# Narrow bias tiles stored from buffers of their own, and seven-plus-one squares in the norms of a two-block transformer kernel

## The reference

```
cond = silu(c); mod = cond @ ada_w + ada_b            # shift, scale, gate
h = rms_norm(x, g) * (1 + scale) + shift              # before every mixer and every MLP
x = x + gate * mixer(h)                               # MLA, dilated, HGRN2 + RWKV7, Fourier + conv
x = x + gate * mlp(h)
rms_norm(x) = x / sqrt(mean(x*x) + eps) * g
```

## Time and profile before

| | us |
|---|---|
| median of 3 runs | 3524.82 (3521.92 to 3530.64) |
| profiled execution | 3524.06 |
| its span in the trace | 3522.1 |
| PE busy | 3307.0 (94%) |
| DVE busy | 1956.5 (56%) |
| POOL busy | 1273.3 (36%) |
| ACT busy | 1256.2 (36%) |

### The profile page before, as it was taken

One profiled execution on the slowest core, in us unless ns is written; L12 is line 12 of the kernel. 1 busy time (PEld: TensorE's weight loads), 2 busy tenths in 40 slices (PEclk: granted clock), 3 DMA queues, 4 the chain that ended last, 5 costly groups with the idle time before them and its releaser, 6 DMA issues.

```text
span 3522.1 us, 62638 instructions
## 1 busy us (share of the span) xinstructions
PE 3307.0 (94%) x25340; PEld 2564.3 (73%) x25340; DVE 1956.5 (56%) x2460; ACT 1256.2 (36%) x2175; POOL 1273.3 (36%) x729
## 2 busy tenths in 40 slices
PE   6799999999989999999999998888999999999998
PEld 4455678887766767778887887666678787578876
DVE  8457566554463555565565665454366465853344
ACT  3345432224554555522224433332322224242222
POOL 0044334445655544334443321000335443034442
PEclk9899999999999999999999998887999999999999
DMA  6433135443434333245442220000255343023322
GB/s 237 116 90 115 59 128 193 157 167 111 130 102 117 111 94 96 69 151 170 168 167 81 58 69 16 4 4 10 66 175 191 119 167 109 16 80 96 95 90 84
DMA packets 278074, 376.46 MB, mean 107 GB/s; under 512 B 59830, under 2 KB 204890, under 8 KB 266586
## 3 DMA queue, kind: packets, MB, share of 16 engines
q1 hardware_dynamic: 273496, 359.31, 32.2%
q10 hardware_dynamic: 4354, 13.98, 1.0%
HBM read 357.49 MB, written 15.73 MB: 106 GB/s over the span
## 4 chain that ended last, share of the span: by engine, by line
PE 77%; DVE 8%; issue 6%; DVEq 2%; ACT 2%; POOL 1%; DMA 1%; SPq 0%; ACTq 0%; POOLq 0%
PE ps L522 14%; PE ps L523 13%; PE ps L526 13%; PE ps L1876 2%; PE ps L1878 2%; PE ps L1877 2%; PE ps L2861 1%; PE ps L1173 1%; PE ps L2862 1%; PE ps L2863 1%; PE ps L1089 1%; PE ps L1906 1%; PE ps L1908 1%; PE ps L1907 1%; DVEq L2680 1%
## 5 line engine op out<-in xcount | busy, mean ns | idle before, releaser
L510 POOL TENSOR_TENSOR w_lo<-w_raw,w_hi 128x1024 fp32r<-128x1024 f32 x288 | 708.7, 2461 | 1050.8 <-ACT w_hi L501 1050.8
L522 PE MATMUL ps<-h_hi,w_hi 128*128 128x512 f32 x2304 | 907.7, 394 | 36.9 <-ACT h_hi L705 13.5
L523 PE MATMUL ps<-h_hi,w_lo 128*128 128x512 f32 x2304 | 904.7, 393 | 0.0
L526 PE MATMUL ps<-h_lo,w_hi 128*128 128x512 f32 x2304 | 826.0, 392 | 0.0
L501 ACT ACTIVATE w_hi<-w_raw 128x1024 fp32r<-128x1024 f32 x288 | 305.5, 1061 | 1111.4 <-PE ps L526 1069.1
L522 PEld LDWEIGHTS ps<-h_hi,w_hi 128*128 128x128 f32 x2304 | 437.6, 190 | 137.4 <-issue 27.1
L523 PEld LDWEIGHTS ps<-h_hi,w_lo 128*128 128x128 f32 x2304 | 437.8, 190 | 90.8
L526 PEld LDWEIGHTS ps<-h_lo,w_hi 128*128 128x128 f32 x2304 | 436.5, 189 | 91.9
L1803 POOL TENSOR_TENSOR w_lo<-w_raw,w_hi 128x512 fp32r<-128x512 f32 x208 | 270.2, 1313 | 329.8 <-ACT w_hi L2069 327.8
L859 DVE TENSOR_TENSOR h_lo<-big,h_hi 128x512 fp32r<-128x512 f32 x100 | 243.0, 2430 | 229.7 <-ACT h_hi L501 229.7
L663 DVE SCALAR_TENSOR_TENSOR big<-yT,cond,big 128x2048 f32<-128x2048 f32 x63 | 176.3, 2798 | 93.5 <-DMA yT<-in_ada_w 93.1
(11 more groups left out here) (505 smaller groups left out, 5697.4 us busy)
## 6 DMA issues: line engine op xcount, KB each, us to landing
w_raw<-in_mlp_w SPq DMA_DIRECT2D x128, 512.0 KB, 3.6
yT<-in_ada_w SPq DMA_DIRECT2D x56, 1024.0 KB, 5.9
w_raw<-in_dil_w_in SPq DMA_DIRECT2D x192, 256.0 KB, 3.1
w_raw<-in_ffn_w_up SPq DMA_DIRECT2D x176, 256.0 KB, 3.1
h_free<-in_ada_w SPq DMA_DIRECT2D x24, 1024.0 KB, 5.6
w_raw<-in_ffn_w_down SPq DMA_DIRECT2D x44, 512.0 KB, 3.5
w_raw<-in_ab_w_in SPq DMA_DIRECT2D x70, 256.0 KB, 2.9
yT<-in_ada_w SPq DMA_DIRECT2D x32, 512.0 KB, 6.3
```

Source lines behind the costliest of these rows:

```text
L510: self.nc.gpsimd.tensor_tensor(self.w_lo[:, s, :], self.w_raw[:, s, :], self.w_hi[:, s, :].bitcast(F32), ALU.subtract).then_inc(sg["w_spli ...
L522: self.nc.tensor.matmul(out, w_hi, h_hi, start=start, stop=False)
L523: self.nc.tensor.matmul(out, w_lo, h_hi, start=False, stop=False)
L526: return self.nc.tensor.matmul(out, self.w_hi[:, s, lo:lo + P], self.h_lo[:, h, :], start=False, stop=stop)
```

## The change

Three parts.

1. The eight narrow bias tiles get a buffer each (`narrow_out`), in space that the start block no longer reads. ACT no longer waits for a store before it copies a narrow tile. The waits for the last stores leave the end of the start block and stand, for all 12 stores of either semaphore, in the mixer behind it: on ACT before its first square of the latents, on DVE before its first copy behind `sin_cos`, and on SP before the dilated mixer reads the bias back.
2. In every norm seven squares instead of eight go through the 32-column products. The eighth goes through a full 128-column product straight into the combined bank, and the combining product adds to it. To make the two fit, DVE's copy becomes a multiplication by 1/32 and Ln's scale becomes 1/D. In the modulation norms the four sums between the squares and the combining product move behind it, so that 6 stand before and 10 behind.
3. The table load moves to the head of the norm. Two norms (`early=4`: behind the dilated mixer and behind the RWKV mixer) square four tiles before they round the first unit.

```diff
+        narrow_out = [self.work(n, (256,)) for n in (22016, 22272, 64, 320, 576, 1024, 1280, 1536)]
...
-                    if x >= 2:
+                    stage = narrow_out[p] if g == 2 else bias_out[x % 2]
+                    if x >= 2 and g < 2:
                         act.wait_ge(sg[f"bias_stored{x % 2}"], sg.at(f"bias_stored{x % 2}", 16 * (x // 2)))
...
-                for u in range(2):
-                    act.wait_ge(sg[f"bias_stored{u}"], sg.at(f"bias_stored{u}", 16 * (len(tiles) // 2)))
...
+            nc.scalar.preload_act_table_set(LN_EXP)
+            squares(0, early)
             for unit in begun:
                 unit(act)
...
+            squares(early, KT)
             for unit in between:
                 unit(act)
-            nc.scalar.preload_act_table_set(LN_EXP)
             act.wait_ge(sg["sums"], sg.at("sums", 1))
-            nc.scalar.activation(self.rs[:], self.ps[:, (bank + 1) % KT, :], ACT.Ln, scale=1.0 / (32 * D), bias=self.eps[:, 0:1])
+            nc.scalar.activation(self.rs[:], self.ps[:, (bank + 1) % KT, :], ACT.Ln, scale=1.0 / D, bias=self.eps[:, 0:1])
...
-            for k in range(4, KT):
+            for k in range(4, KT - 1):
                 last = part(k)
             last.then_inc(sg["parts"], 1)
-            if ada is not None:
-                self.ada_sums(pe, ada_bank, 6, 10, ada, False)
+            pe.wait_ge(sg["squares"], sg.at("squares", KT))
+            nc.tensor.matmul(self.ps[:, (bank + 1) % KT, :], self.c["ones"][:], self.yT[:, KT - 1, :], start=True, stop=False)
             pe.wait_ge(sg["parts_in"], sg.at("parts_in", 1))
...
-                self.ada_sums(pe, ada_bank, 10, 16, ada)
+                self.ada_sums(pe, ada_bank, 6, 16, ada)
...
-            nc.vector.tensor_copy(self.yT[:, 0, :], self.ps[:, bank, :]).then_inc(sg["parts_in"], 1)
+            nc.vector.tensor_scalar(self.yT[:, 0, :], self.ps[:, bank, :], 1.0 / 32, None, ALU.mult).then_inc(sg["parts_in"], 1)
```

More of the change, by code:

```diff
@@ L449, in start @@
                 points=len(tiles), padded=1, x_squared=KT, x_summed=KT,
[L450 to L451 removed]
+                bias_full=before(len(tiles)), bias_copied=before(len(tiles)))
     def _loop(self, eng, first, end, body):
@@ L674, in first_units, with norm_after @@
         return unit[:1], unit[1:2], {4: unit[2]}
-    def norm_after(self, block, g, layer, sub, bank, split, ada=None, ahead=None, ada_more=None, lo=None):
+    def norm_after(self, block, g, layer, sub, bank, split, ada=None, ahead=None, ada_more=None, lo=None, early=0):
         nc, sg = self.nc, self.sg
@@ L689, in _, with squares @@
             begun, between, among = ahead or ([], [], {})
+            def squares(first, end):
+                for k in range(first, end):
+                    act.wait_ge(sg["out_free"], sg.at("out_free", KT + k + 1))
+                    nc.scalar.activation(self.yT[:, k, :], self.xT[:, k, :], ACT.Square).then_inc(sg["squares"], 1)
+            nc.scalar.preload_act_table_set(LN_EXP)
+            squares(0, early)
             for unit in begun:
                 unit(act)
-            for k in range(KT):
-                act.wait_ge(sg["out_free"], sg.at("out_free", KT + k + 1))
-                nc.scalar.activation(self.yT[:, k, :], self.xT[:, k, :], ACT.Square).then_inc(sg["squares"], 1)
+            squares(early, KT)
             for unit in between:
                 unit(act)
-            nc.scalar.preload_act_table_set(LN_EXP)
             act.wait_ge(sg["sums"], sg.at("sums", 1))
-            nc.scalar.activation(self.rs[:], self.ps[:, (bank + 1) % KT, :], ACT.Ln, scale=1.0 / (32 * D), bias=self.eps[:, 0:1])
+            nc.scalar.activation(self.rs[:], self.ps[:, (bank + 1) % KT, :], ACT.Ln, scale=1.0 / D, bias=self.eps[:, 0:1])
             act.drain()
@@ L1269, in _ @@
             nc.scalar.preload_act_table_set(LN_EXP)
+            for u in range(2):
+                act.wait_ge(sg[f"bias_stored{u}"], sg.at(f"bias_stored{u}", 16 * 12))
             for m in range(5):
@@ L1417, in _ @@
             nc.vector.tensor_scalar(t_turn, t_turn, -1.0, math.pi / 2, ALU.mult, ALU.add).then_inc(sg["angles"], 1)
+            for u in range(2):
+                v.wait_ge(sg[f"bias_stored{u}"], sg.at(f"bias_stored{u}", 16 * 12))
             v.wait_ge(sg["sin_cos"], sg.at("sin_cos", 1))
@@ L1747, in _ @@
                 load(n)
+            for u in range(2):
+                sp.wait_ge(sg[f"bias_stored{u}"], sg.at(f"bias_stored{u}", 16 * 12))
             sp.wait_ge(sg["ada_sum"], sg.at("ada_sum", 0))
@@ L4077, in build @@
             k.dilated(block)
-            k.norm_after(block, k.col("norm_mlp", KT, KT), 1, 1, 2, True, ahead=k.first_units())
+            k.norm_after(block, k.col("norm_mlp", KT, KT), 1, 1, 2, True, ahead=k.first_units(), early=4)
             k.mlp(block, 1, Ada(2, 12))
@@ L4082, in build @@
             k.rwkv(block)
-            k.norm_after(block, k.col("norm_g_2", KT, KT), 2, 1, 0, True, ahead=k.first_units(2))
+            k.norm_after(block, k.col("norm_g_2", KT, KT), 2, 1, 0, True, ahead=k.first_units(2), early=4)
             k.conv_ffn(block, 2, Ada(3, 16))
```

10 lines of the change are left out of this document (5 added, 5 removed).

## The result

The changed kernel takes 3519.93 us (median of 20 runs, 3512.38 to 3530.11), the kernel before, beside it, 3528.69 (20 runs, 3521.92 to 3536.68). The ratio is 0.9973, with a 95% interval from 0.9965 to 0.9982: 9.5 us less, between 6 and 12 (the medians differ by 8.8). The forecast was 11.4 us less than the 3524.8 shown, 3513.4, with a range up to 3519.0. The direction was right and the time lies outside the range, by 0.9 us. Most of the 6.5 us between forecast and time is the starting point: the three runs of before lay low in that kernel's own spread. The rest is the start block, which gave less than forecast in most executions.

A forecast was written before the change was run, and what follows sets the result against it. PE, busy 94% of the span, bounds the kernel. Start -7.2, clock -0.8, plain norms -1.8, early-square norms -3.5, modulation norms +2.2 make -11.1 us: 3524.06 to 3513.0, median 3513.7, forecast 3513.4; range 3509.0 to 3519.0.

The forecast's parts named there:

- The level: Whole kernel: starting from the profiled execution's 3524.06 us, the change gives 3513.0; the median is 0.8 higher, 3513.7.
- The start: End of the start block: without the store waits the next block begins at 109.8, not 116.95, 7.2 us less.
- The rival of slow issues: Start block: ACT's queue backs up, each of eight store issues takes 3.1 us more, total 3538 us; chance 0.04.
- the barrier: End of the start block: the barrier before the next block itself takes about 0.5 us.
- the start gives only part: Start block: DMA traffic leaves some 4 of the 7.2 us, no clock gain, total 3517 to 3518; chance 0.07.
- The clock behind the start: Mixer behind the start block: PE's shorter gap shortens the half-speed stretch, -0.8 us, between 0 and -2.5.
- a stretch at 0.50 of less than 5 us: Behind the start block: sign that the forecast is right, PE's granted clock at 0.50 for less than 5 us.
- The rival of a clock that comes back wholly: Behind the start block: a 3 us gap costs no slow stretch, -2.5 instead of -0.8, total 3511.7; chance 0.09.
- The norms: Eight norms: three without modulation -1.8 us together, two with early squares -3.5 together, three with modulation +2.2 together.
- the norms give nothing: Eight norms: the full eighth product costs more than a square's time, norms sum to +0.6, total 3517 us; chance 0.10.

The follow-up runs named there:

- e2_norms: The kernel before with the change's new norms only, start block and store waits as before: 3520.79 us, ratio 0.9998 to the kernel before.
- after_fourth: The changed kernel itself, unaltered, in a further execution beside the kernel before: 3517.95 us, ratio 0.9964.
- e9_old_late: The changed kernel with all three modulation norms in the order of before, and eight modulation sums made twice behind the second one's combining product: 3526.67 us.
- e8_second_old: The changed kernel with the order of before in the second modulation norm alone: 3525.17 us, 0.7 above the changed kernel.
- e6_start_fill: The changed kernel with unread full products in the start block, three before the last two wide tiles and one before the third narrow tile: 3522.47 us.

## Why the prediction was wrong in its time and right in its cause

**The level.** This is the step that failed: "Against the profiled execution, 3524.06 [...], this is 3513.0. The median is 0.8 higher, which gives 3513.7", and with it the range that "reaches from 3509.0 (all terms near their good bound) to 3519.0". It holds the errors of the terms and none of the starting point. The three runs shown were the first of twenty whose median is 3528.69, 3.9 above theirs. The same 11.4 from there is 3517.3. Of the 6.5 us between 3513.4 and 3519.93, the level is thus 3.9; the other 2.6 are the difference, 8.8 between the medians instead of 11.4, and the step behind those is the start below. Neither alone would have left the range. (3513.4 is also 0.3 under the sum's own 3513.7, and the prediction gives no reason for it.) A kernel whose single runs spread by 4 to 6 us, and whose median moves by up to 9.5 with the chip, has no level known to within 1 us from three runs, and a single profiled execution's is known no better.

**The start: the mechanism right, the size too sure.** The rival of slow issues is refuted (0.33 to 0.60 us each in the first profile of the change, 0.76 at most in any). The waits that moved to the mixer cost nothing that any profile shows, and the barrier takes 0.43 us (112.48 to 112.91), where I put 0.5. But the one profile of before had PE's sums at 3.67 us, and I took PE's share as fixed: this is the term of the sum that was mis-sized, "The next block begins at 109.8 in place of 116.95: 7.2 us less". With the store waits the block ended at 116.95 and 116.79, in two profiles that both had short sums (3.67 and 3.63), so it is not shown what long ones would do there. Without the waits PE ends the block, and it is up to 3.5 us later than I had it, by the clock. Over the thirteen executions with own buffers and no products in the start the next block begins at 111.85 on average (109.41 to 113.29): 5.0 less instead of 7.2. My rival "the start gives only part" came near that size by luck: its cause was DMA traffic, and here it was PE's clock.

**The clock behind the start** was -0.8, with 0 to -2.5. From the next block's begin to the first Ln it took 353.1 us before and 353.9 in e2_norms; the four profiles of the change have 349.5, 353.5, 349.8 and 354.4, 351.8 on average. With the norm's 0.67 taken off the first of these, that is 0.6 less than before, and it is 2.1 less than e2_norms: about -1, with more spread than size. The cause that I gave is not borne out. I named a stretch at 0.50 of less than 5 us as its sign. Behind the start of the mixer the first profile of the change has 0.50 from 114 to 119 and 0.86 from 119 to 124, no shorter than before; after_fourth has it shorter (0.79 from 114 to 119), and so has e2_norms (0.72 from 119 to 124), whose start is the old one. The rival of a clock that comes back wholly falls with these windows.

**The norms** came out as worked out: -0.67 each (I had -0.6), -1.82 and -1.77 (-1.75), +0.87 (+0.75). In the modulation norms the three 32-column products took 0.99 us (822.61 to 823.60), as four had, where I put 0.95, and from the first of the twenty records behind the combining product to DVE's addition it is 2.33 us (825.43 to 827.76), where I put 2.08. The full product took 0.96 to the next one (823.60 to 824.56), so the change of width shows no cost. e2_norms gives the time of all this, 2.0 less, so times cannot exclude the rival "the norms give nothing"; by rows it is refuted.

**What the trace holds back:** the expected sum, corrected, is -5.0 - 1 - 3.0 = -9.0. The four comparisons have -8.8, -10.4, -7.8 and -12.5 in their medians, and -10.0 ±1.7 by their means, weighted by their precision. That agrees with -9.0, and it does not exclude the 11.4 either: that the start gives less than 7.2 rests on the profiles, not on the times. The first pair of profiles had 0.9 because the recurrent stage lasted 9 us longer by its clock in that execution.

## What to carry to other kernels

Work out a level's uncertainty as you work out the terms: with three runs of a kernel that spreads by 5 us, the forecast of a time needs some 5 us either way, though the forecast of the difference may be far sharper. Where a wait is removed from a chain, look at how far the new last engine varies between executions, since it now sets the end. And the idle gap in the first norm cost PE twice, once idle and once at a low clock behind it; unread products that fitted into the gap delayed nothing. Whether such products shorten the whole kernel has to be measured: in the norms they did together with the old modulation order, and in the start block they did not.

## What the runs showed of the hardware that was not expected

PE's granted clock fell while PE was busy without a break, in one-column products: 0.73 from 1862 to 1867 in e9_old_late with PE busy for all 5.00 us, and 0.50 from 103.4 to 106.8 in the change with PE busy for 3.40 of 3.40. At full clock 32 records of them took 3.63 us, and up to 6.23 (e8_second_old) where a stretch at 0.50 covered them. Filling the longest idle time ahead of them did not prevent it (0.50 from 103.4 to 106.8 in e6_start_fill). That it is the small products that let the clock fall is not shown: no run has others in their place. The same kernel's median differs by up to 0.27% between chips (3522.81 to 3532.28), and the mean granted clock with it (0.9610 to 0.9589). Neither is shown to be the other's whole cause.
